# The second MLP's down projection wholly by 7 block products, in parts of 10, 10 and 12 tiles

## The chip, the cores and the metric

One core of one Trainium2 chip. The metric is the device time of one execution in microseconds, as the median of the runs.

## What is computed

Two transformer layers of the older kind (an "even" one with differential and dense attention, an "odd" one with window attention), a final norm, and then one hybrid layer with dilated attention, a state space model and gated units. All data is float32; h has 1024 features and 512 tokens (528 with the meta tokens). The change lies in the odd layer's MLP and at its seam to the hybrid layer:

```python
def _sq_relu_mlp(h, w_up, w_down):
    u = jax.nn.relu(h @ w_up)
    return (u * u) @ w_down

h = h + _sq_relu_mlp(_rmsnorm(h, norm_mlp[i]), w_up[i], w_down[i])    # 1024 -> 4096 -> 1024
h = _rmsnorm(h, norm_final)
return h[:, N_META:]

# the hybrid layer begins with
n = rmsnorm(h, g_mix)
z = n @ w_in
```

## The kernel before

Everything is stored with the features on the 128 partitions and the tokens along a row, so h is 8 tiles of 128x512 (`DT = 8`). A float32 product is made of three matmuls in a rounded type: each operand is split into a rounded half (`_hi`) and the rest (`_lo`), and hi x hi, hi x lo and lo x hi are added in PSUM. A **unit** is one weight tile of 8 x 128x128. SP loads it to `raw` (ring of 4), ScalarE rounds it to `w_hi` (ring of 2, `round_unit`), GpSimd subtracts to get `w_lo` (ring of 2, `low`), TensorE runs 24 matmuls on it. Each engine has its program written out by hand in one function; semaphores with counts tie them together. Nothing reorders the work afterwards.

The second MLP (of the odd layer) has 32 inner tiles of 128. Before, they are treated in two parts of 12 (`up_parts`, `MLP_PARTS = 2`, `PART_SIZES`) and a rest of 8 (`last_up`, `last_down`). For a part:
- *Up.* `project(pj)` makes each inner tile by one unit. VectorE takes it from PSUM with relu and the scale `rstd`, ScalarE squares and rounds it (`round_inner`), VectorE makes four sums of each pair of tiles (`sums_of_pair`), and both split them (`sums_high`, `sums_low`) to `form_hi`, `form_lo`.
- *Down.* `down_by_products` on TensorE, `by_products` on ScalarE and VectorE. The output is treated in four **quads** (`Quad`), each two tiles of h by the two halves of the tokens. A quad is 7 products P1, P2, P5, P6, P3, P4, P7, in this order, in place of the 8 of a 2x2 block product. A product is, for every pair of inner tiles, three matmuls of 128x256: 15 in a part of 10 tiles, 18 in one of 12. Its weights are a block of the matrix or a sum of blocks (VectorE, `weight_sum`), rounded by ScalarE (`product_high`), with the rest by VectorE (`product_low`) or, for P3 and P4, by GpSimd. They lie in a ring of three: `third_hi`/`third_lo` and the two slots of `w_hi`/`w_lo`. VectorE adds each product to h (`keep`).
- In the first quad of a part the last pair of inner tiles is late. So TensorE takes P1, then P2 and P5 with all but the last pair, then the last pair of both.
- `BEHIND[part]` is the unit that follows the part: ScalarE rounds it once the product P3 of the last quad is done (`round_unit`), and the next once P4 is done (`held`).

The rest of 8 tiles is plain. `last_up` makes 8 units into `mr_hi`, `mr_lo`; `last_down` makes the 8 tiles of h with 24 matmuls of 128x512 each. With each finished tile of h, `residual(last_down, 40, True, twice=True)` has ScalarE scale and round it for the hybrid layer (`norm_tile`, L2079) and take two squares of it, with and without the final norm's gain (L2073, L2115). VectorE makes `hr_lo` (L2872) and adds up `sumsq` and `sumsq2` (L2882, L2938). The hybrid layer's projection `middle` starts with `H_LO`, which means that its first unit waits tile by tile for `hr_lo`. Behind this unit `both_stats` adds the squares over the partitions with two matmuls against `ones`; ScalarE's root and VectorE's reciprocal of it scale all that follows. The hybrid layer's gated MLP uses the same block products, in parts of 10 and 12 (`ffn_in`, `ffn_rest`). Its last part already rounds h between its products (`round_residual`, `low_residual`).

## Time and profile before

| | us |
|---|---|
| median of 3 runs | 2095.23 |
| lowest, highest | 2095.11, 2095.38 |
| the profiled execution | 2094.85 |
| its span on the core | 2092.7 |

| engine | busy us | share of the span | instructions |
|---|---|---|---|
| TensorE, matmuls | 2079.1 | 99% | 14278 |
| VectorE | 1355.1 | 65% | 2083 |
| ScalarE | 879.5 | 42% | 1454 |
| GpSimd | 829.0 | 40% | 388 |

The busy time is that of the engine's instructions laid over each other; the span runs from the first instruction to the last. Matmuls are pipelined, so the duration of one in a row is longer than its share of the time: what one costs is the distance between the starts of neighbours. In brackets behind a row stands how long the engine was idle before it, and what it waited for.

### The profile page before, as it was taken

The numbers are of one execution on the slowest core, as the hardware profiler recorded it, in microseconds if no ns is written. First come the engines' busy times: TensorE is split into PE (matmuls) and PEld (weight loads), VectorE is DVE, ScalarE is ACT, GpSimd is POOL, SyncE is SP. The second block draws the span as 40 slices with busy tenths as digits, with TensorE's granted clock in tenths as the row PEclk, the third lists the DMA queues.
The fourth block names the chain that finished last, engine by engine and source line by source line (L and its number), as shares of the span: only waits on it lengthen the run. The fifth ranks groups of instructions, "written<-read, shape, count | busy, mean of one in ns | idle before, by whom it ended". The sixth has DMA issues, their size and how long they took to land.

```text
span 2092.7 us, 35077 instructions
## 1 busy us (share of the span) xinstructions
PE 2079.1 (99%) x14278; PEld 1826.3 (87%) x14278; DVE 1355.1 (65%) x2083; ACT 879.5 (42%) x1454; POOL 829.0 (40%) x388
## 2 busy tenths in 40 slices
PE   9999999999999999999999999999999999999998
PEld 9998899999999777798898788888888788988897
DVE  6678766625723395675855769576774577666865
ACT  5368644223323493443434423344433433433344
POOL 3343434434444453423234443333434443344332
PEclk9999999999999999999999999999999999999999
DMA  6620245233433602323343465233333332433341
GB/s 180 168 59 2 57 136 150 88 117 105 136 91 102 180 2 81 101 87 106 85 117 97 131 136 159 71 84 89 88 91 91 91 94 79 122 91 100 89 122 61
DMA packets 375695, 211.18 MB, mean 101 GB/s; under 512 B 26915, under 2 KB 368132, under 8 KB 374648
## 3 DMA queue, kind: packets, MB, share of 16 engines
q1 hardware_dynamic: 365230, 192.62, 32.6%
q10 hardware_dynamic: 10314, 16.41, 2.8%
q8 instruction: 111, 1.82, 0.4%
q14 instruction: 40, 0.33, 0.1%
HBM read 196.97 MB, written 15.40 MB: 101 GB/s over the span
## 4 chain that ended last, share of the span: by engine, by line
PE 65%; issue 22%; POOL 10%; DVE 2%; ACT 0%; DMA 0%; POOLq 0%; SPq 0%; DVEq 0%; ACTq 0%
PE acc L1268 15%; PE acc L1269 15%; PE acc L1270 14%; POOL w_lo L1038 9%; PE acc L1358 2%; PE ops L1427 2%; PE acc L1679 1%; PE acc L1671 1%; PE acc L1669 1%; PE tps L1367 1%; PE acc L1141 1%; PE ops L1421 1%; PE acc L1142 1%; PE acc L1143 1%; PE tps L1679 1%
## 5 line engine op out<-in xcount | busy, mean ns | idle before, releaser
L1038 POOL TENSOR_TENSOR w_lo<-raw,w_hi 128x1024 fp32r<-128x1024 f32 x278 | 688.2, 2476 | 964.8 <-ACT w_hi L1999 954.3
L1999 ACT ACTIVATE w_hi<-raw 128x1024 fp32r<-128x1024 f32 x277 | 293.4, 1059 | 839.9 <-PE acc L1270 810.5
L1268 PE MATMUL acc<-hr_hi,w_hi 128*128 128x512 f32 x1056 | 421.5, 399 | 0.3 <-POOL w_lo L1038 0.3
L1270 PE MATMUL acc<-hr_hi,w_lo 128*128 128x512 f32 x1056 | 417.7, 396 | 0.0
L1269 PE MATMUL acc<-hr_lo,w_hi 128*128 128x512 f32 x1056 | 417.6, 395 | 0.0
L1268 PE MATMUL acc<-hn_hi,w_hi 128*128 128x264 f32 (+1 forms) x840 | 246.8, 294 | 0.4 <-POOL w_lo L1038 0.4
L1270 PE MATMUL acc<-hn_hi,w_lo 128*128 128x264 f32 (+1 forms) x840 | 244.2, 291 | 0.0
L1269 PE MATMUL acc<-hn_lo,w_hi 128*128 128x264 f32 (+1 forms) x840 | 244.2, 291 | 0.0
L1268 PEld LDWEIGHTS acc<-hr_hi,w_hi 128*128 128x128 f32 x1056 | 198.5, 188 | 48.6 <-issue 1.5
L1270 PEld LDWEIGHTS acc<-hr_hi,w_lo 128*128 128x128 f32 x1056 | 198.4, 188 | 47.9
L1269 PEld LDWEIGHTS acc<-hr_lo,w_hi 128*128 128x128 f32 x1056 | 198.5, 188 | 47.1 <-issue 0.7
L1268 PEld LDWEIGHTS acc<-hn_hi,w_hi 128*128 128x128 f32 x840 | 158.2, 188 | 3.4 <-issue 0.5
L1269 PEld LDWEIGHTS acc<-hn_lo,w_hi 128*128 128x128 f32 x840 | 158.3, 188 | 2.7
L1270 PEld LDWEIGHTS acc<-hn_hi,w_lo 128*128 128x128 f32 x840 | 157.5, 188 | 2.4
L1268 PE MATMUL acc<-mid_hi,w_hi 128*128 128x264 f32 x512 | 145.5, 284 | 0.0
L1269 PE MATMUL acc<-mid_lo,w_hi 128*128 128x264 f32 x512 | 145.0, 283 | 0.0
L1270 PE MATMUL acc<-mid_hi,w_lo 128*128 128x264 f32 x512 | 145.0, 283 | 0.0
L1102 POOL TENSOR_TENSOR w_lo<-blocks,w_hi 128x768 fp32r<-128x768 f32 (+1 forms) x24 | 44.3, 1852 | 138.7 <-ACT w_hi L2404 138.7
L1268 PEld LDWEIGHTS acc<-mid_hi,w_hi 128*128 128x128 f32 x512 | 96.4, 188 | 0.2 <-issue 0.2
L1269 PEld LDWEIGHTS acc<-mid_lo,w_hi 128*128 128x128 f32 x512 | 96.5, 188 | 0.0
L1270 PEld LDWEIGHTS acc<-mid_hi,w_lo 128*128 128x128 f32 x512 | 96.0, 187 | 0.0
L2404 ACT ACTIVATE w_hi<-blocks 128x768 fp32r<-128x768 f32 (+1 forms) x72 | 59.0, 823 | 87.7 <-PE acc L1679 26.9
(551 smaller groups left out, 4389.0 us busy)
## 6 DMA issues: line engine op xcount, KB each, us to landing
raw<-in_w_up SPq DMA_DIRECT2D x64, 512.0 KB, 4.4
raw<-in_w_in SPq DMA_DIRECT2D x56, 512.0 KB, 3.8
raw<-in_w_down SPq DMA_DIRECT2D x40, 512.0 KB, 3.6
blocks<-in_w_down SPq DMA_DIRECT2D x32, 384.0 KB, 3.4
raw<-in_w_ffn_gate SPq DMA_DIRECT2D x22, 512.0 KB, 3.9
raw<-in_w_ffn_up SPq DMA_DIRECT2D x22, 512.0 KB, 3.8
raw<-in_w_in_even SPq DMA_DIRECT2D x18, 512.0 KB, 6.9
blocks<-in_w_ffn_down SPq DMA_DIRECT2D x16, 384.0 KB, 3.5
```

What stands on the lines that cost most here:

```text
L1038: nc.gpsimd.tensor_tensor(w_lo[:, part], raw[:, slot], w_hi[:, part].bitcast(F32), ALU.subtract).then_inc(sems["lo"], T.up("lo"))
L1102: nc.gpsimd.tensor_tensor(lo, block_of(q, PRODUCTS[i][0]), hi.bitcast(F32), ALU.subtract).then_inc(sems["product_lo_pool"], 1)
L1141: mm(out, w_hi[:, part, k, :], x_hi, start=first, stop=False)
L1142: mm(out, w_hi[:, part, k, :], x_lo, start=False, stop=False)
L1268: mm(out, w_hi[:, part, w0 + k, :], xh, start=s0, stop=False)
L1269: mm(out, w_hi[:, part, w0 + k, :], xl, start=False, stop=False)
L1270: ins = mm(out, w_lo[:, part, w0 + k, :], xh, start=False, stop=s1)
L1358: ins = mm(bank[rows, c:c + w], q, keys, start=first, stop=last)
L1427: ins = mm(ops_[b][rows, to], p.v[o][k], weights(o, k)[:, queries], start=k == 0, stop=k == last)
L1679: ins = mm(region(q, i), lo[:, k, :], form_hi[:, form, k, :], start=False, stop=k == pairs - 1, skip_group_check=not opens)
L1999: fn(w_hi[:, n % 2], raw[:, n % 4], ACT.Copy).then_inc(sems["hi"], T.up("hi"))
L2404: fn(weights_of(q, i)[0], block_of(q, role), ACT.Copy).then_inc(sems["product_hi"], 1)
```

## The change

- `PART_SIZES` becomes (10, 10, 12, 10, 12) with `MLP_PARTS = 3`. `last_up` and `last_down` and their buffers are gone: all 32 inner tiles go through block products.
- In the first quad of every part, also of the gated MLP's two, P6's rounded half with all but the last pair comes ahead of the last pairs of P2 and P5; ScalarE rounds P6's weights ahead of the last `sums_high`.
- The third part (`NORM_PART`) does between its products what `last_down` did per tile: scaled rounding of the quad before (`round_gained`, `low_gained`), squares two tiles at a time (`plain_squares`, `gained_squares`) and their sums (`add_plain`, `add_gained`, `fold`). The square tiles lie in `hid_2` and in parts of `form_hi` and `form_lo` that have been read for the last time.
- Behind this part ScalarE rounds two units at once, before the last rounding of h.
- The two matmuls against `ones` move from behind `middle`'s first unit into its second: one ahead of the second k-step, one ahead of the fifth.

```diff
-MLP_PARTS = 2
-PART_SIZES = (PART_TILES, PART_TILES, 10, PART_TILES)
+MLP_PARTS = 3
+PART_SIZES = (10, 10, PART_TILES, 10, PART_TILES)
+NORM_PART, FFN_PART, LAST_PART = MLP_PARTS - 1, MLP_PARTS, MLP_PARTS + 1
...
@@ TensorE
                         for i in (P2, P5):
                             open_product(q, i)
                             high(q, i, most)
                             low(q, i, most)
+                        open_product(q, P6)
+                        high(q, P6, most)
                         for i in (P2, P5):
                             high(q, i, rest)
                             low(q, i, rest)
+                        high(q, P6, rest)
+                        low(q, P6, range(pairs))
...
-            project(last_up)
-            project(last_down, None, ("hidden_lo", LAST_TILES))
...
-            project(middle, None, H_LO, both_stats, after_tile=middle_after)
+            def both_stats(k):
+
+                if k == 1:
+                    pe.wait_ge(sems["gained_sum"], DT // 2)
+                    b = open_("o_")
+                    close(mm(ops_[b][:], ones[:], gained_sums[:, 0], start=True, stop=True), b, "o_")
+                if k == 4:
+                    pe.wait_ge(sems["plain_sum"], DT // 2)
+                    b = open_("o_")
+                    close(mm(ops_[b][:], ones[:], plain_sums[:, 0], start=True, stop=True), b, "o_")
+
+            project(middle, None, H_LO, ahead=[None, both_stats], after_tile=middle_after)
@@ ScalarE
+            def round_gained(q):
+
+                act.wait_ge(sems["product_kept"], q.done(P7))
+                for m in (q.n, q.n + 1):
+                    fn(hr_hi[:, m, :], h[:, m, 0:SEQ], ACT.Copy, scale=gains[:, 40 + m:41 + m]).then_inc(
+                        sems["h_hi"], T.up("h_hi"))
+
+            def plain_squares(n):
+
+                fn(plain[n], h[:, 2 * n:2 * n + 2, 0:SEQ], ACT.Square).then_inc(sems["plain_square"], 1)
...
+            def norm_between(q, i):
+
+                if i == P5 and not q.first:
+                    round_gained(q.before)
+                    if not q.last:
+                        plain_squares(q.n // 2 - 1)
+                if q.last and i == P6:
+                    gained_squares(0)
+                if q.last and i == P3:
+                    gained_squares(1)
+                if q.last and i == P4:
+                    plain_squares(2)
+                if q.last and i == P7:
+                    gained_squares(2)
...
                 act.wait_ge(sems["product"], own[-1].done(P7) - 2)
                 round_unit(BEHIND[part])
-                held[BEHIND[part] + 1] = own[-1].done(P7) - 1
+                if part == NORM_PART:
+                    act.wait_ge(sems["product"], own[-1].done(P7) - 1)
+                    round_unit(BEHIND[part] + 1)
+                    early.append(True)
+                    round_gained(own[-1])
+                    gained_squares(3)
+                    plain_squares(3)
+                else:
+                    held[BEHIND[part] + 1] = own[-1].done(P7) - 1
@@ VectorE
+            def add_gained(n):
+
+                dve.wait_ge(sems["gained_square"], 2 * n + 2)
+                if n > 1:
+                    dve.wait_ge(sems["gained_sum"], n - 1)
+                v.tensor_tensor(gained_sums, gained_sums, gained[n], ALU.add).then_inc(sems["gained_sum"], 1)
...
                     keep(q, P3)
+                    if part == NORM_PART and q.last:
+                        add_plain(1)
...
                     keep(q, P4)
...
+                    if part == NORM_PART and q.last:
+                        add_gained(1)
+                        add_gained(2)
                     keep(q, P7)
+                    if part == NORM_PART and q.last:
+                        add_plain(2)
+                        low_gained(q)
+                        add_gained(3)
+                        fold(gained_sums, "gained_sum")
+                        add_plain(3)
+                        fold(plain_sums, "plain_sum")
```

The order on VectorE at the seam. Before, from the last two tiles of `last_down` to the hybrid layer's first scaling (`acc` is PSUM, `u_t` the first tile of the hybrid layer):

```order
L2929 TENSOR_TENSOR h<-h,acc0 128x512
L2872 SCALAR_TENSOR_TENSOR hr_lo<-h,gains,hr_hi 128x512
L2882 TENSOR_TENSOR sumsq<-sumsq,sq 128x512
L2938 TENSOR_TENSOR sumsq2<-sumsq2,sq2 128x512
L2929 TENSOR_TENSOR h<-h,acc1 128x512
L2872 SCALAR_TENSOR_TENSOR hr_lo<-h,gains,hr_hi 128x512
L2882 TENSOR_TENSOR sumsq<-sumsq,sq 128x512
L2938 TENSOR_TENSOR sumsq2<-sumsq2,sq2 128x512
L3670 RECIPROCAL rstd<-rstd 128x512
L3761 TENSOR_TENSOR u_t<-acc0,rstd 128x64x8
```

In the change, from the keep of P3 in the last quad of the third part (`ops0` is P3's PSUM, `tps` P4's, `acc1` P7's; `hid_2` and `gained0` hold the running sums):

```order
L3541 TENSOR_TENSOR h<-h,ops0 128x256
L3594 TENSOR_TENSOR hid_2<-hid_2 128x1024
L3541 TENSOR_TENSOR h<-h,tps 128x256
L3601 TENSOR_TENSOR gained0<-gained0,gained1 128x1024
L3601 TENSOR_TENSOR gained0<-gained0,gained2 128x1024
L3541 TENSOR_TENSOR h<-h,acc1 128x2x256
L3594 TENSOR_TENSOR hid_2<-hid_2,plain1 128x1024
L3585 SCALAR_TENSOR_TENSOR hr_lo<-h,gains,hr_hi 128x512 x2
L3601 TENSOR_TENSOR gained0<-gained0,gained3 128x1024
L3606 TENSOR_TENSOR gained0<-gained0 128x512
L3594 TENSOR_TENSOR hid_2<-hid_2,plain2 128x1024
L3606 TENSOR_TENSOR hid_2<-hid_2 128x512
```

The two adds of `gained` stand between the keeps of P4 and P7, and one add of `hid_2` between the keep of P7 and the last `hr_lo`.

On ScalarE at the same place, before (each tile: a unit's weights, `hr_hi`, two squares):

```order
L1999 ACTIVATE w_hi<-raw 128x1024
L2079 ACTIVATE hr_hi<-h,gains 128x512
L2073 ACTIVATE sq<-h 128x512
L2115 ACTIVATE sq2<-h,gains 128x512
L2079 ACTIVATE hr_hi<-h,gains 128x512
L2073 ACTIVATE sq<-h 128x512
L2115 ACTIVATE sq2<-h,gains 128x512
L1999 ACTIVATE w_hi<-raw 128x1024
L2676 ACTIVATE rstd<-ops0,small 128x512
L2676 ACTIVATE sq<-ops1,small 128x512
```

and in the change, from the weights of P6 in the last quad on:

```order
L2393 ACTIVATE third_hi<-blocks 128x768
L2428 ACTIVATE gained0<-h,gains 128x512 x2
L2393 ACTIVATE w_hi<-blocks 128x768
L2428 ACTIVATE gained1<-h,gains 128x512 x2
L2393 ACTIVATE w_hi<-blocks 128x768
L2423 ACTIVATE plain1<-h 128x1024
L2393 ACTIVATE third_hi<-blocks 128x768
L2428 ACTIVATE gained2<-h,gains 128x512 x2
L1997 ACTIVATE w_hi<-raw 128x1024 x2
L2418 ACTIVATE hr_hi<-h,gains 128x512 x2
L2428 ACTIVATE gained3<-h,gains 128x512 x2
L2423 ACTIVATE plain2<-h 128x1024
```

The weights of two units now come ahead of the last two `hr_hi`, and squares stand behind each product's weights.

On TensorE in the first quad of a part, from the end of P5's first pairs (`tps` is P2, `ops` P5, `acc` P6), before:

```order
L1679 MATMUL ops<-form_hi,w_lo 128x256 x5
L1669 MATMUL tps<-form_hi,w_hi 128x256
L1671 MATMUL tps<-form_lo,w_hi 128x256
L1679 MATMUL tps<-form_hi,w_lo 128x256
L1669 MATMUL ops<-form_hi,w_hi 128x256
L1671 MATMUL ops<-form_lo,w_hi 128x256
L1679 MATMUL ops<-form_hi,w_lo 128x256
L1669 MATMUL acc<-form_hi,third_hi 128x256
L1671 MATMUL acc<-form_lo,third_hi 128x256
```

and in the change, with the end of P6's first pairs:

```order
L1664 MATMUL acc<-form_hi,third_hi 128x256
L1666 MATMUL acc<-form_lo,third_hi 128x256
L1664 MATMUL acc<-form_hi,third_hi 128x256
L1666 MATMUL acc<-form_lo,third_hi 128x256
L1664 MATMUL tps<-form_hi,w_hi 128x256
L1666 MATMUL tps<-form_lo,w_hi 128x256
L1674 MATMUL tps<-form_hi,w_lo 128x256
L1664 MATMUL ops<-form_hi,w_hi 128x256
L1666 MATMUL ops<-form_lo,w_hi 128x256
L1674 MATMUL ops<-form_hi,w_lo 128x256
L1664 MATMUL acc<-form_hi,third_hi 128x256
L1666 MATMUL acc<-form_lo,third_hi 128x256
```

The last pairs of P2 and P5 now come behind P6's rounded half instead of ahead of it.

## Rows read from the trace of the kernel before

**Rows 1.** The page: its first line, and part 1, busy time by engine

```profile
span 2092.7 us, 35077 instructions
...
PE 2079.1 (99%) x14278; PEld 1826.3 (87%) x14278; DVE 1355.1 (65%) x2083; ACT 879.5 (42%) x1454; POOL 829.0 (40%) x388
```

**Rows 2.** The waits of TensorE, whole span: us in total, times, longest

```profile
PE acc L1268 <- POOL w_lo L1038: 1.1, 3, 0.4
...
PE ops L1669 <- DVE form_lo L3530: 0.8, 1, 0.8
```

**Rows 3.** Busy time by stretch (columns: see the second line)

```profile
core 0: us, PE busy (x) PEld busy (x) DVE busy (x) ACT busy (x) POOL busy (x), PEclk, DMA share, GB/s
902.64:962.16 59.52, 59.52 (x505) 59.52 (x504) 41.38 (x65) 26.21 (x31) 17.71 (x10) 1.00 0.39 109
...
1133.71:1178.49 44.78, 44.78 (x193) 36.06 (x192) 33.43 (x32) 21.87 (x31) 19.26 (x8) 1.00 0.32 93
1776.49:1827.36 50.87, 49.77 (x421) 49.36 (x420) 38.01 (x66) 22.93 (x30) 15.63 (x10) 1.00 0.41 113
```

**Rows 4.** Timeline, TensorE, first quad of the gated part (start, us, engine, line, ...)

```profile
1781.43 0.28 PE L1679 MATMUL tps<-form_hi,w_lo 128*128 128x256 f32 x1
1782.55 0.39 PE L1669 MATMUL ops<-form_hi,w_hi 128*128 128x256 f32 x1 [0.85 <-DVE form_lo L3530]
```

**Rows 5.** Timeline, VectorE, same quad

```profile
1781.28 1.22 DVE L3530 TENSOR_TENSOR form_lo<-pair_sums,form_hi 128x1024 fp32r<-128x1024 f32 x1
1782.42 0.82 DVE L3506 TENSOR_TENSOR third_lo<-blocks,third_hi 128x640 fp32r<-128x640 f32 x1
```

**Rows 6.** Timeline, TensorE: first matmul behind the second part, and behind the gated part

```profile
1088.91 0.39 PE L1268 MATMUL acc<-hr_hi,w_hi 128*128 128x512 f32 x1
...
1827.37 0.47 PE L1268 MATMUL acc<-hr_hi,w_hi 128*128 128x512 f32 x1 [0.26 <-POOL w_lo L1038]
```

**Rows 7.** Timeline, ScalarE, end of the second part

```profile
1084.87 1.06 ACT L1999 ACTIVATE w_hi<-raw 128x1024 fp32r<-128x1024 f32 x1 [1.23 <-PE ops L1679]
1086.99 1.06 ACT L1999 ACTIVATE w_hi<-raw 128x1024 fp32r<-128x1024 f32 x1 [1.06 <-PE tps L1679]
```

**Rows 8.** Timeline, GpSimd, end of the second part

```profile
1086.01 4.78 POOL L1038 TENSOR_TENSOR w_lo<-raw,w_hi 128x1024 fp32r<-128x1024 f32 x2 [2.54 <-ACT w_hi L1999]
```

**Rows 9.** Timeline, VectorE, end of the second part

```profile
1084.87 0.42 DVE L3525 TENSOR_TENSOR h<-h,ops 128x256 f32<-128x256 f32 x1 [0.24 <-PE ops L1679]
1086.99 0.42 DVE L3525 TENSOR_TENSOR h<-h,tps 128x256 f32<-128x256 f32 x1 [1.70 <-PE tps L1679]
1089.11 0.69 DVE L3525 TENSOR_TENSOR h<-h,acc 128x512 f32<-128x512 f32 x1 [1.70 <-PE acc L1679]
```

**Rows 10.** Timeline, VectorE, then GpSimd, one up projection

```profile
1014.81 2.58 DVE L3530 TENSOR_TENSOR form_lo<-pair_sums,form_hi 128x1024 fp32r<-128x1024 f32 x1 [1.35 <-ACT form_hi L2409]
...
1026.19 1.21 DVE L3530 TENSOR_TENSOR form_lo<-pair_sums,form_hi 128x1024 fp32r<-128x1024 f32 x1
...
1013.90 2.41 POOL L1038 TENSOR_TENSOR w_lo<-raw,w_hi 128x1024 fp32r<-128x1024 f32 x1 [3.20 <-ACT w_hi L1999]
```

**Rows 11.** Timeline, VectorE, then GpSimd, end of the gated up projections

```profile
1945.84 4.03 DVE L3499 TENSOR_TENSOR blocks<-blocks 128x768 f32<-128x768 f32 x2
...
1946.37 2.68 POOL L1038 TENSOR_TENSOR w_lo<-raw,w_hi 128x1024 fp32r<-128x1024 f32 x1 [3.07 <-ACT w_hi L1999]
```

**Rows 12.** Timeline, VectorE, then GpSimd, second quad of the second gated part

```profile
1981.39 1.22 DVE L3560 TENSOR_TENSOR hr_lo<-h,hr_hi 128x1024 fp32r<-128x1024 f32 x1
1982.53 0.95 DVE L3506 TENSOR_TENSOR w_lo<-blocks,w_hi 128x768 fp32r<-128x768 f32 x1
...
1982.42 2.76 POOL L1102 TENSOR_TENSOR w_lo<-blocks,w_hi 128x768 fp32r<-128x768 f32 x1 [9.71 <-ACT w_hi L2404]
```

**Rows 13.** Timeline, ScalarE, then VectorE, last tile of last_down

```profile
1179.43 0.72 ACT L2079 ACTIVATE hr_hi<-h,gains 128x512 fp32r<-128x512 f32 x1 [3.52 <-DVE h L2929]
...
1180.18 0.75 DVE L2872 SCALAR_TENSOR_TENSOR hr_lo<-h,gains,hr_hi 128x512 fp32r<-128x512 f32 x1 [0.79 <-ACT hr_hi L2079]
```

More of the change, by code:

```diff
@@ L495, in transposed_blocks_program @@
             att_lo = sb(s, "att_lo", [P, 4, SEQ], F32R)
+        FORM, FORMS_LO = PART_PAIRS * SEQ // 2, 7 * PART_PAIRS * SEQ // 2
+        gained = [over(at, (f"gained{n}", [P, 2, SEQ]))[0] for n, at in enumerate((SEQ, FORMS_LO, FORM, 2 * FORM))]
+        plain = [plain_sums, hid_2[:, 0]] + [over(FORMS_LO + n * FORM, (f"plain{n}", [P, 2, SEQ]))[0] for n in (1, 2)]
+        gained_sums = gained[0]
         bb, = over(34 * LEN, ("bb", [P, 2, 16, 16]))
@@ L2757, in middle_tile @@
                     fn(mixed_hi[:, n, :], G[:, 0, :], ACT.Copy).then_inc(sems["mixed_hi"], T.up("mixed_hi"))
-            project(middle, middle_tile, own=[t for t, x in enumerate(MID) if x[0] == "glu_b"], first=both_stats)
+            project(middle, middle_tile, own=[t for t, x in enumerate(MID) if x[0] == "glu_b"], second=both_stats)
             residual(out_2, 48, True)
@@ L3587, in by_products @@
                             low_residual(q.before)
+                        if part == NORM_PART:
+                            low_gained(q.before)
                     product_low(q, P6)
```

113 lines of the change are left out of this document (41 added, 72 removed).

## Prediction

> **What bounds the kernel now.** I read the page's totals first: TensorE is busy 99% of a 2092.7 us span [rows 1]. The list of waits on that engine then says how much of the span it stands still at all. In the whole kernel it has one wait of 0.8 us for a `form_lo` tile and three of 1.1 us together for a `w_lo` tile [rows 2]; the rest is as small. So time comes off this kernel only where TensorE gets fewer or shorter instructions, and anything on VectorE, ScalarE or GpSimd costs nothing until a matmul waits for it. The table of stretches prices the two kinds of matmul. The granted clock is 1.00 (2.4 GHz) in all of them. 504 block matmuls of 256 columns took 59.52 us, 0.1181 us each, and the 192 plain matmuls of `last_down` took 44.78 us, 0.2333 us each [rows 3]. The ten-tile part of the gated MLP is the one place where the block form already shows stalls: 50.87 us for 420 matmuls, where 420 x 0.1181 is 49.60, so 1.3 us are waits [rows 3].
>
> **The change, part by part.** In what follows M is the moment at which the layer behind a part starts on TensorE (1088.91 behind the second part of before [rows 6]).
>
> *Matmuls.* The up projections keep 32 tiles. The down product had 2 x 504 block matmuls and 192 plain ones. Now it has 420 + 420 + 504 = 1344 block matmuls. Added: 336 x 0.1181 = 39.7 us. Removed: 44.8 us. Net -5.1 us, all on the path. The two sums with `ones` stay, two products of two passes each, only later in the program: 0.
>
> The Trainium skill speaks against this trade: TensorE: Matmul & The Clock Gate, section Back-to-back issue gap, gives about 81 ns for a sustained matmul of 128 columns with its weight load and 131 ns for one of 512, so that halving the columns saves far less than half. An estimate between its two figures, 98 ns at 256 columns, would make this part 336 x 0.098 - 192 x 0.131 = +7.8 us. The trace disagrees with it at both widths [rows 3], and the measurement decides.
>
> *Ends of the ten-tile parts.* ScalarE rounds the next unit's weights once the product P3 is done and GpSimd subtracts behind it. In a twelve-tile part this starts 4.04 us before M [rows 7, 6] and the first GpSimd subtraction, half of 4.78 us from M - 2.90, ends 0.5 us before it is needed [rows 8]. With ten tiles the two products behind P3 last 0.7 us less (2 x 3 matmuls), and the first matmul behind the gated part did wait 0.26 us for that subtraction [rows 6]. I take 0.35 us for each of parts one and two (0.26 to 0.5): +0.7 us.
>
> *First quads.* P6's rounded half with all but the last pair now runs ahead of the last pairs of P2 and P5. That covers 8 matmuls, 0.9 us, in a ten-tile part. The gated part waited 0.85 us for `form_lo` (with the slower matmuls about it, 1.0) [rows 4, 5]. With the cover, the low part of P6 is next: VectorE's subtraction for it runs 0.82 us from 1782.42 [rows 5], to 6.8 us behind the start, and TensorE wants it at 6.5. So that part gets back about 0.6 of its 1.0 us. What is pushed back is the end of P2, and with it ScalarE's rounding and GpSimd's 1.6 to 1.85 us subtraction for P3. In a ten-tile MLP part I work this out as 0.25 us of wait. In a twelve-tile one P2 now ends 1.2 us later and P3's low part is some 0.4 us late where nothing was late before. Parts: +0.25 +0.25 +0.35 (the third), -0.6 (first gated), +0.1 (second gated): +0.3 us, between -0.6 and +1.5.
>
> *Inside the third part's quads.* For each quad ScalarE gets two scaled roundings (0.72 us each by the row of `hr_hi` [rows 13]) and about 1.06 us of squares behind P5's weights. It has 2.1 us for each product and needs 0.85 for its weights, so P6's weights start at most 0.8 us late with more than 2 us in hand: 0. VectorE gets two `hr_lo` of 0.75 us where the second gated part has one of 1.22 us [rows 12, 13], 0.3 us more. P6's subtraction then stands near the moment at which GpSimd asks for its own [rows 12]. I take +0.2 us for all quads (0 to 1.8).
>
> *From the last quad into the next layer.* Here is the largest unknown. VectorE and GpSimd do not overlap when both read two SBUF operands. A 128x1024 subtraction takes 1.21 us alone and 2.58 us when it begins 0.9 us into GpSimd's 2.41 us: it ended 1.1 us behind GpSimd's end [rows 10]. Additions into PSUM-fed `h` are untouched beside GpSimd, at 0.42 us [rows 9, 8]. The order in VectorE's program is now: keep P3, add squares (1024 wide), keep P4, two more such adds, keep P7, one more add, then the two `hr_lo`. Placed on the rows of before:
> - keep P3 is at M - 4.0, so the first add runs from M - 3.7 to M - 2.5. GpSimd asks at M - 2.9 and holds the port from M - 2.5 to M - 0.1: just in time for TensorE.
> - keep P4 is at M - 1.9 [rows 9]. The second add comes at M - 1.6, finds the port taken and ends at M + 1.0.
> - GpSimd's next subtraction has been ready since M - 0.1. Where VectorE issued a second two-operand instruction while GpSimd already asked, GpSimd went in between (two 0.95 us instructions took 4.03 us [rows 11]). So: GpSimd to M + 3.4, the third add to M + 4.5, and keep P7 to M + 5.1 where it was done at M + 0.9 [rows 9].
> - ScalarE's `hr_hi` of the last two tiles follow at M + 5.8 and M + 6.4; VectorE's add and `hr_lo` end at M + 6.9 and M + 7.6.
> - TensorE wants the seventh tile after 18 matmuls, at M + 4.2. It waits 2.8 us. The sum of squares (two roundings, two squares, an add, a fold) is ready at M + 9.5 and wanted at M + 9.1: 0.4 us more.
>
> If VectorE holds the port for both adds instead, keep P7 ends at M + 2.7, but then the add before `hr_lo` runs into GpSimd, and the same chain gives 2.1 + 0.4 us. I take +3.0 us (0 if nothing meets on the port, 3.4 at most).
>
> The Trainium skill, SBUF — State Buffer, section Who interferes with whom, says that whichever of the two issues first gets the shared port pair for its whole instruction. By that rule the waiting second add goes ahead of GpSimd's next subtraction and the third behind it, which is the first of my two orders; no row of before shows GpSimd with two in a row and VectorE waiting. The sum by the rule would be 0.2 us above mine.
>
> **Sum:** -5.1 + 0.7 + 0.3 + 0.2 + 3.0 = -0.9 us. The profiled execution took 2094.85 us, its span 2092.7; so 2093.95. The median of the runs is 2095.23, 0.38 above it: I forecast 2094.3.
>
> **Rivals.**
> - *No meeting on the port (chance 0.25).* For it: every add is only 1.2 us and stands in a gap of 1.7 us between two keeps. Against: GpSimd's 2.4 us fills that gap. Without it keep P7 ends at M + 0.9, the add at M + 2.0 and the `hr_lo` at M + 2.7 and M + 3.4, ahead of the 4.2 and 4.9 at which they are wanted, and the squares' sum at M + 5.2 ahead of 6.3. -5.1 + 0.7 + 0.3 + 0.1 = -4.0: 2091.2.
> - *The full arithmetic (0.05).* Early P6 also clears the new first-quad waits and the part ends cost little: -5.1, 2090.1.
> - *Slower: VectorE loses the port in the quads too (0.12).* If its subtraction for P6 is asked for more than about 0.2 us behind GpSimd's for P3, it waits for 1.85 us. In the second gated part the two lie 0.11 us apart [rows 12], and the new quads bring 0.3 us more work ahead of it. P6's low half would be 0.6 us late in each of three quads (+1.8 for +0.2), the first quads 0.8 us worse, the end 0.4 us worse. It makes -0.9 + 1.6 + 0.8 + 0.4 = +1.9: 2097.1. It decides from the point where these waits together pass 5.1 us.
> - *It does not do what it says:* the built order shows the plain matmuls gone and the squares in the quads, so no chance.
>
> **How the numbers follow.** The forecast with its own spread (2093.3 to 2095.3) has 0.58. The range reaches over the no-meeting case and half of the slower one: 2090.9 to 2096.2. A measurement of this kernel can tell about 0.2%, 4.2 us, from no change. The no-meeting case at -4.0 is on that line: two fifths of it and the full arithmetic, with a little for errors of mine, make 0.17 for faster. Slower by 4.2 us needs the slower case and more: 0.03. The rest, 0.80, is within.
>
> **What would show it.** Right: TensorE's wait list gains one of 2 to 3 us for `hr_lo` in the layer's first unit and a shorter one for the squares' sum; VectorE's two adds of `gained` take 2 us and more each; keep P7 starts 2 to 4 us late; the 420-matmul stretches last 50.2 us. Wrong: if `hr_lo` is never waited for, the port chain was wrong and the time is near 2091; if the quads of the third part last over 60.5 us, the slower rival holds; if block matmuls are not at 0.118 us, the first term is wrong.

## The result, and the profile of the changed kernel

| | before | changed |
|---|---|---|
| median of 20 runs each, same chip | 2095.17 us | 2097.59 us |
| ratio, 95% interval | | 1.0014 [1.0008, 1.0021] |
| profiled execution, span | 2094.85, 2092.7 us | 2097.81, 2096.0 us |

The change made the kernel 2.4 us slower. By the 0.2% that I called the smallest difference to be told it is no change; the interval is narrower than that and lies wholly above 1. The forecast was 2094.3, the range ended at 2096.2, so the time is outside it. The profile shows one execution of each kernel, so its spans differ by 3.3 us where the medians differ by 2.4.

The first rows of the page, against [rows 1]: TensorE is busy 0.4 us longer, though its matmuls should last 5.1 us less, and the span is 3.3 us longer. So most of the loss lies in what counts as busy.

```profile
span 2096.0 us, 35502 instructions
...
PE 2079.5 (99%) x14422; PEld 1831.6 (87%) x14422; DVE 1383.7 (66%) x2149; ACT 891.2 (43%) x1474; POOL 829.2 (40%) x388
```

The waits of TensorE, whole span (us in total, times, longest). The `form_lo` wait of [rows 2] is gone. A wait of 2.3 us for `hr_lo` is new. So are short ones for weights (`w_lo` at L1033 and L1097) and for `h`.

```profile
PE acc L1263 <- DVE hr_lo L3585: 2.3, 1, 2.3
...
PE acc L1263 <- POOL w_lo L1033: 1.0, 5, 0.2
...
PE ops L1674 <- POOL w_lo L1097: 0.4, 2, 0.2
...
PE acc L1664 <- DVE h L3541: 0.3, 1, 0.3
```

The table of stretches: the three parts of the second MLP (compare [rows 3]), then four stretches at the start of the layer behind them (its first matmul is at 1176.54, the M of the forecast).

```profile
core 0: us, PE busy (x) PEld busy (x) DVE busy (x) ACT busy (x) POOL busy (x), PEclk, DMA share, GB/s
891.49:942.26 50.77, 50.46 (x421) 49.80 (x420) 37.16 (x65) 23.35 (x31) 15.64 (x10) 1.00 0.42 114
998.34:1049.09 50.75, 50.44 (x421) 49.78 (x420) 37.16 (x65) 23.35 (x31) 15.65 (x10) 1.00 0.43 114
1116.36:1176.54 60.18, 59.90 (x505) 59.51 (x504) 48.47 (x73) 35.97 (x46) 20.91 (x10) 1.00 0.39 108
...
1180.60:1183.30 2.70, 0.38 (x2) 0.00 (x0) 2.70 (x5) 1.80 (x3) 0.00 (x0) 1.00 0.68 194
1183.30:1184.60 1.30, 1.28 (x5) 1.02 (x6) 1.13 (x2) 1.30 (x3) 0.00 (x0) 0.97 0.00 0
1184.60:1187.30 2.70, 2.70 (x8) 1.69 (x6) 2.63 (x4) 1.47 (x2) 0.85 (x1) 0.50 0.03 6
1187.30:1190.00 2.70, 2.70 (x11) 1.75 (x9) 2.70 (x2) 0.69 (x1) 2.12 (x1) 0.88 0.00 0
```

What to see: the down product took 50.77 + 50.75 + 60.18 = 161.7 us. Before it was 59.54 + 59.55 + 44.80 = 163.9 (the first two are 504 matmuls each, as in [rows 3]). That is 2.2 us less, where 5.1 us less of matmul time was forecast. 1344 x 0.118 is 158.6, so 3.1 us are waits. Then one matmul starts at 1180.58 and the next at 1183.32: TensorE is idle for 2.34 us. It starts again at full clock, and 1.3 us later the granted clock falls to 0.50 (1.2 GHz) for 2.7 us. Below I call this stop the gap; the recorded texts count it as 2.7 us, from start to start.

From M to the first transposes of the new layer there are 192 matmuls of eight units. They lasted from 1178.50 to 1225.01 before, 46.51 us, and from 1176.54 to 1228.08 now, 51.54 us: 5.03 us more. The first transposes, before and now:

```profile
1225.01 0.60 PE L1328 MATMUL tps<-ident,qkv 128*128 128x128 f32 x4
...
1228.08 0.60 PE L1323 MATMUL tps<-ident,qkv 128*128 128x128 f32 x4
```

The two parts of the gated MLP took 0.15 and 0.22 us more. Together -2.2 + 5.0 + 0.4 = +3.2 of the span's 3.3 us.

TensorE at that place (start, us, engine, line, ...):

```profile
1183.32 0.50 PE L1263 MATMUL acc<-hr_hi,w_hi 128*128 128x512 f32 x1 [2.34 <-DVE hr_lo L3585]
...
1185.08 0.63 PE L1263 MATMUL acc<-hr_hi,w_hi 128*128 128x512 f32 x1
...
1186.36 1.80 PE L1884 MATMUL ops<-gained,ones 128*128 128x512 f32 x2
1187.28 1.11 PE L1263 MATMUL acc<-hr_hi,w_hi 128*128 128x512 f32 x1
...
1190.09 1.06 PE L1888 MATMUL ops<-hid,ones 128*128 128x512 f32 x2
...
1194.37 0.50 PE L1263 MATMUL acc<-hr_hi,w_hi 128*128 128x512 f32 x1 [0.43 <-DVE u_t L3806]
```

VectorE, then GpSimd, in the same stretch:

```profile
1174.73 6.13 DVE L3601 TENSOR_TENSOR gained<-gained 128x1024 f32<-128x1024 f32 x2
1180.79 0.68 DVE L3541 TENSOR_TENSOR h<-h,acc 128x512 f32<-128x512 f32 x1
...
1182.52 1.40 DVE L3585 SCALAR_TENSOR_TENSOR hr_lo<-h,gains,hr_hi 128x512 fp32r<-128x512 f32 x2
...
1185.36 0.69 DVE L3606 TENSOR_TENSOR gained<-gained 128x512 f32<-128x512 f32 x1
1185.97 1.22 DVE L3594 TENSOR_TENSOR hid<-hid,plain 128x1024 f32<-128x1024 f32 x1
1187.22 2.75 DVE L3606 TENSOR_TENSOR hid<-hid 128x512 f32<-128x512 f32 x1
1189.89 3.34 DVE L3715 RECIPROCAL rstd<-rstd 128x512 f32<-128x512 f32 x1
1193.27 1.05 DVE L3806 TENSOR_TENSOR u_t<-acc,rstd 128x512 f32<-128x512 f32 x1
...
1173.41 6.37 POOL L1033 TENSOR_TENSOR w_lo<-raw,w_hi 128x1024 fp32r<-128x1024 f32 x2 [1.53 <-ACT w_hi L1997]
...
1186.45 2.97 POOL L1033 TENSOR_TENSOR w_lo<-raw,w_hi 128x1024 fp32r<-128x1024 f32 x1 [6.67 <-ACT w_hi L1997]
```

The first row is the forecast meeting: two adds of 1.2 us took 6.13 us beside two subtractions of GpSimd that took 6.37 instead of 4.78 [rows 8]. The rest of the list is what I did not follow to its end: behind the gained fold come a plain add and the plain fold, the fold 2.75 us for its 0.69 beside GpSimd's next subtraction, and only then the reciprocal that every `u_t` needs. The third unit of the layer waits for the first `u_t`, since it takes over that tile's accumulator. The same two steps in the kernel before, and the start of its third unit on TensorE:

```profile
1185.88 3.35 DVE L3670 RECIPROCAL rstd<-rstd 128x512 f32<-128x512 f32 x1 [3.74 <-ACT rstd L2676]
1189.27 1.09 DVE L3761 TENSOR_TENSOR u_t<-acc,rstd 128x512 f32<-128x512 f32 x1
...
1191.41 0.40 PE L1268 MATMUL acc<-hr_hi,w_hi 128*128 128x512 f32 x1
```

There the first `u_t` was done at 1190.36 and the third unit began at 1191.41: 1.05 us in hand. Behind M the reciprocal ended at +10.73 (1185.88 + 3.35 - 1178.50) before and at +16.69 now, 5.96 us later. Less the 1.05 in hand that is 4.9 us, the seam's loss to 0.1 us. That the third unit starts behind the first `u_t` is in the row; the experiments had to show whether the time follows from it, or from the gap and the clock.

### The profile page after: what moved, and what is told of

Read it like the earlier page. It is cut to its first block, busy times and chain, and to the rows that moved or that the text cites. A ratio compares the mean times of both kernels' runs of the same rounds, so it can differ in the third digit from the quotient of the medians.

```text
span 2096.0 us, 35502 instructions
## 1 busy us (share of the span) xinstructions
PE 2079.5 (99%) x14422; PEld 1831.6 (87%) x14422; DVE 1383.7 (66%) x2149; ACT 891.2 (43%) x1474; POOL 829.2 (40%) x388
## 4 chain that ended last, share of the span: by engine, by line
PE 66%; issue 20%; POOL 10%; DVE 3%; ACT 1%; POOLq 0%; DMA 0%; DVEq 0%; ACTq 0%
PE acc L1263 15%; PE acc L1264 15%; PE acc L1265 15%; POOL w_lo L1033 8%; PE acc L1353 2%; PE ops L1422 2%; POOL w_lo L1097 1%; PE acc L1664 1%; PE acc L1666 1%; PE tps L1362 1%; PE ops L1416 1%; PE acc L1136 1%; PE acc L1674 1%; PE acc L1138 1%; PE acc L1137 1%
## 5 line engine op out<-in xcount | busy, mean ns | idle before, releaser
L1033 POOL TENSOR_TENSOR w_lo<-raw,w_hi 128x1024 fp32r<-128x1024 f32 x270 | 671.6, 2488 | 937.6 <-ACT w_hi L1997 926.8
L1997 ACT ACTIVATE w_hi<-raw 128x1024 fp32r<-128x1024 f32 x269 | 285.2, 1060 | 810.5 <-PE acc L1265 778.5
L1097 POOL TENSOR_TENSOR w_lo<-blocks,w_hi 128x640 fp32r<-128x640 f32 (+1 forms) x30 | 56.5, 1893 | 165.6 <-ACT w_hi L2393 165.6
L2393 ACT ACTIVATE w_hi<-blocks 128x640 fp32r<-128x640 f32 (+1 forms) x90 | 70.0, 784 | 108.3 <-PE acc L1674 24.0
```

The costliest lines, as they stand in the source:

```text
L1033: nc.gpsimd.tensor_tensor(w_lo[:, part], raw[:, slot], w_hi[:, part].bitcast(F32), ALU.subtract).then_inc(sems["lo"], T.up("lo"))
L1097: nc.gpsimd.tensor_tensor(lo, block_of(q, PRODUCTS[i][0]), hi.bitcast(F32), ALU.subtract).then_inc(sems["product_lo_pool"], 1)
L1997: fn(w_hi[:, n % 2], raw[:, n % 4], ACT.Copy).then_inc(sems["hi"], T.up("hi"))
L2393: fn(weights_of(q, i)[0], block_of(q, role), ACT.Copy).then_inc(sems["product_hi"], 1)
```

## The experiments

Each was timed in 11 runs, the kernel before 21 or 33 times on the same chip, with medians of 2094.85 to 2095.09. The ratios are to that kernel. Experiments 1 to 4, 5 to 8, 9 and 10, and 11 and 12 were made on four different chips, and the changed kernel was not timed again beside them: a difference to its 2097.59 goes across chips. All intervals are some 0.09% (1.9 us) to either side, so smaller differences of the medians rest on the traces.

**1. The two adds ahead of P7's keep left out** (the gained sum is then without the squares of four tiles; the counts that wait for these adds are lowered to fit).

```diff
-                    if part == NORM_PART and q.last:
-                        add_gained(1)
-                        add_gained(2)
```

> The change without VectorE's two adds of gained squares between the keeps of P4 and P7 in the third part's last quad; their terms are missing from one sum of squares. Port theory (these two adds wait behind GpSimd and so hold back the keep of P7 and the last hr_lo): the 2.7 us gap in the hybrid layer's first unit goes, and with it the matmuls at 0.43 us and the late start of the third unit, some 4.5 to 5 us in all: about 2093. Rival (the chain from the last product over ScalarE's rounding to hr_lo is itself too long to be covered by six tiles of matmuls): a gap of 1.5 us or more stays, 2096 or more.

Measured: 2094.97 us, ratio 0.9999 [0.9990, 1.0008]. The gap before the seventh tile and the slow matmuls are gone. So the two adds, with all that their meeting with GpSimd brings, cost 2.6 us by the medians and 3.0 us at the seam (first transposes at M + 48.57 for 51.54). The run takes out the adds and the meeting together and does not price them apart. The time stayed 2 us above the 2093 expected: the third unit still waited, because the reciprocal still came late, behind the plain sums:

```profile
1184.18 2.77 DVE L3604 TENSOR_TENSOR hid<-hid 128x512 f32<-128x512 f32 x1
1186.88 3.34 DVE L3710 RECIPROCAL rstd<-rstd 128x512 f32<-128x512 f32 x1
```

**2. P6 of the first quads in its place of before.**

```diff
-                        open_product(q, P6)
-                        high(q, P6, most)
                         for i in (P2, P5):
                             high(q, i, rest)
                             low(q, i, rest)
-                        high(q, P6, rest)
-                        low(q, P6, range(pairs))
...
-                        whole(q, P6)
-                    for i in (P3, P4, P7):
+                    for i in (P6, P3, P4, P7):
```

ScalarE's rounding of P6's weights goes back behind the last `sums_high` with it.

> The change with the order of the first quads of before: P6 behind the last pairs of P2 and P5. Theory of the forecast (early P6 covers the wait for form_lo in ten-tile parts): without it each ten-tile part loses about 0.6 us, the twelve-tile parts win 0.3 to 0.4 each: +1.1 us net, 2098.7. Rival, from the trace of the change (what it covers comes back as a wait for P3's low half and for the second quad's P2): ten-tile parts within 0.2 us of the change, twelve-tile parts 0.4 us less each, 2096.8.

Measured: 2096.86 us, ratio 1.0008 [0.9999, 1.0017]. The quads took 50.85, 50.55 and 59.54 us, against 50.77, 50.75 and 60.18. So with ten tiles the early P6 takes away one wait for `form_lo` (0.60 us idle, 0.86 with the slower matmuls about it) and gives the same back: 0.24 us at P3's low weights, 0.40 at P2's in the second quad, 0.21 at P5's last pair. With twelve tiles there was nothing to take away, and it costs 0.6 us. That is the rival of the expectation, not the forecast's theory. The ten-tile gated part took 51.19 us here, 51.04 in the changed kernel.

**3. The gap filled with 10 spare matmuls on `ones`.**

```diff
+            def fill(k):
+                if k == 6:
+                    for _ in range(10):
+                        mm(ops_[1][:, 0:P], ones[:], ones[:], start=True, stop=True)
...
-            project(middle, None, H_LO, ahead=[None, both_stats], after_tile=middle_after)
+            project(middle, None, H_LO, ahead=[fill, both_stats], after_tile=middle_after)
```

> The change with 10 spare matmuls of 128 columns against ones (float32, two passes each, into an unused bank) at the place where TensorE waits for the seventh tile's hr_lo. The wait stays as long. Clock theory (the granted clock falls to 1.2 GHz because TensorE stood still): the matmuls behind stay at 0.23 us and the sums against ones at 0.43 us a pass, 1.7 to 2 us less: about 2095.8. Rival (the slow matmuls are no matter of standing still): as slow as in the change, 2097.6, or more by what the spare matmuls outlast the wait.

Measured: 2097.67 us, ratio 1.0015 [1.0006, 1.0024], no gain at all. The table of stretches of this kernel, for the same four stretches:

```profile
1180.60:1183.30 2.70, 2.59 (x22) 2.40 (x21) 2.70 (x5) 2.02 (x4) 0.00 (x0) 1.00 0.67 194
1183.30:1184.60 1.30, 1.30 (x6) 0.99 (x6) 1.12 (x2) 1.30 (x2) 0.00 (x0) 1.00 0.00 0
1184.60:1187.30 2.70, 2.28 (x8) 1.24 (x7) 2.63 (x4) 1.51 (x3) 1.36 (x1) 1.00 0.00 0
```

The clock stays at 1.00, so it was the standing still that had let it fall. The expected 1.7 to 2 us did not come: the matmuls, now faster, came to VectorE's results too early. TensorE in this kernel:

```profile
1185.89 1.12 PE L1884 MATMUL ops<-gained,ones 128*128 128x512 f32 x2 [0.42 <-DVE gained L3612]
...
1189.82 1.12 PE L1888 MATMUL ops<-hid,ones 128*128 128x512 f32 x2 [0.72 <-DVE hid L3612]
...
1194.16 0.50 PE L1263 MATMUL acc<-hr_hi,w_hi 128*128 128x512 f32 x1 [0.43 <-DVE u_t L3812]
```

M is 1176.33 here, so the third unit starts at M + 17.83, to 0.01 us where it started in the changed kernel. The slow clock had cost nothing here: it lay in the shadow of VectorE's chain.

**4. The kernel before, with the early P6 alone.**

> The kernel before with P6 early in the first quads, alone (parts of 12, 12, 10, 12). By the trace of the change: the ten-tile part no better (0.0 to +0.2 us), the three twelve-tile parts 0.3 to 0.45 us longer each: +1.1 us, 2096.3. By the forecast: -0.6 for the ten-tile part and +0.1 to +0.4 for the others: 2095.2 to 2095.6.

Measured: 2096.31 us, ratio 1.0007 [0.9998, 1.0016]; the first two twelve-tile parts took 59.93 us each instead of 59.54, the ten-tile gated part 51.24 instead of 50.89, the last part 49.32 instead of 49.15. In the twelve-tile parts it agrees in sign with the second experiment (0.4 us here; there 0.6, of which 0.2 is a wait at the part's end that these two do not have). In the ten-tile gated part it does not: 0.35 us lost here, 0.15 won there. The early P6 gained nothing in either.

**5. VectorE's order changed, all sums kept.**

```diff
                     keep(q, P3)
-                        add_plain(1)
+                        add_gained(1)
...
                     keep(q, P4)
-                        add_gained(1)
-                        add_gained(2)
                     keep(q, P7)
-                        add_plain(2)
                         low_gained(q)
+                        add_gained(2)
                         add_gained(3)
                         fold(gained_sums, "gained_sum")
+                        add_plain(1)
+                        add_plain(2)
                         add_plain(3)
                         fold(plain_sums, "plain_sum")
```

> All sums are kept; in the last quad of the third part VectorE's order is changed: the first gained add in the place of the first plain one (before GpSimd's two subtractions begin), no add in front of P7's keep, the other two gained adds, the fold, and then all three plain adds and their fold behind the low parts of the residual, ahead of the reciprocal. Port theory (the two adds in front of P7's keep took 6.13 us beside GpSimd and made the 2.7 us gap at k = 6 of the first unit): the gap shrinks to under 0.5 us and no matmul runs at 427 ns. Chain theory (VectorE's whole list of sums, the plain ones with it, stands in front of the reciprocal that u_t needs): the third unit of the middle projection then waits over 2 us for u_t, since four plain additions of some 4.5 us now stand ahead of the reciprocal, and the time is 2096.5 to 2098, no better than the changed kernel. If only the gap counted, it would be 2094.5.

Measured: 2098.19 us, ratio 1.0015 [1.0006, 1.0024]: no better, as the chain theory said, but not where it said. The gap is gone, and the wait stands at the plain ones product (3.3 us), not at the third unit. The reciprocal ends at M + 16.46, 0.2 us earlier than in the changed kernel. Behind the wait the granted clock fell to 0.50 for 2.8 us, against the expectation, and the second unit ended so late that the first `u_t` was done 1.0 us before the third unit began.

**6. The last plain add, the plain fold and the plain ones product behind the first `u_t`.**

```diff
                         fold(gained_sums, "gained_sum")
-                        add_plain(3)
-                        fold(plain_sums, "plain_sum")
...
+                if m == 0:
+                    add_plain(3)
+                    fold(plain_sums, "plain_sum")
```

> The changed kernel with the last plain add and the plain fold behind the reciprocal and the first u_t, and the plain ones product (with its square root) one unit later. Chain theory: the reciprocal starts about 2 to 3 us earlier (the fold of 2.75 us beside GpSimd no longer stands ahead of it), u_t is there in time, the third unit's wait of 0.43 and 0.1 us goes, and the time falls by 0.5 us against the changed kernel; the gap of 2.7 us and the matmuls at 427 ns stay, since the gained adds stand where they stood. Rival (only the gap counts): no difference, within 0.2 us.

The new lines stand in `chunked`, behind the store of `u_t`; the plain ones product moves from the second unit to the third. Measured: 2097.22 us, ratio 1.0010 [1.0001, 1.0019], 0.4 us under the changed kernel; the two intervals overlap, so this alone tells little. The reciprocal starts 1.0 us earlier behind M, not 2 to 3. It now waited for its square root, since the gained ones product ran at the halved clock. By the timeline the clock cost something here; no run tests it. The third unit starts at M + 16.88, 0.95 us earlier, and the first transposes at M + 51.44, only 0.10 earlier: the plain ones product now stands behind the third unit's start and costs its 0.86 us there.

**7. Both edits (5 and 6).**

> Both edits together, all sums kept. Chain theory: neither the gap, nor slow matmuls, nor the wait of the third unit; what is left of the seam are the two interruptions by the ones products (about 0.7 us each): 2097.6 less 2.7 for the gap less about 1 for the slow matmuls and the wait, 2093.5 to 2094.5. Rival (the loss at the seam is the ones products and the waits of the low parts themselves, whatever the order): over 2095.5.

Measured: 2097.31 us, ratio 1.0011 [1.0002, 1.0020]. Expected were 2093.5 to 2094.5, so I had not understood it yet. VectorE of this kernel, then TensorE:

```profile
1184.08 3.23 DVE L3603 TENSOR_TENSOR hid<-hid,plain 128x1024 f32<-128x1024 f32 x1
1187.23 3.34 DVE L3721 RECIPROCAL rstd<-rstd 128x512 f32<-128x512 f32 x1
...
1191.69 0.80 PE L1263 MATMUL acc<-hr_hi,w_hi 128*128 128x512 f32 x1 [2.78 <-DVE u_t L3816]
1192.28 0.63 PE L1264 MATMUL acc<-hr_lo,w_hi 128*128 128x512 f32 x1
```

The gap at the seventh tile is gone, and a stop of the same size stands at the third unit. A plain add met GpSimd's next subtraction and took 3.23 us ahead of the reciprocal, and the slow matmuls came back with the stop (granted clock 0.50 from 1191.7 to 1194.4, seven matmuls, some 1.4 us).

**8. The same with the late P6.**

> The same with P6 of the first quads back in its place of before (the version meant to be the best of both). Since the earlier P6 cost about 0.6 us in the twelve-tile part and something like 0.2 in the others, 0.7 us less than the kernel with both edits: 2092.8 to 2094. That is 1 to 2 us under the kernel before. If the two effects do not add, the same time as with both edits.

Measured: 2096.69 us, ratio 1.0008 [0.9999, 1.0018]. Against its sister 0.6 us less, inside the intervals of both but of the size of experiment 2, and not the level expected (2092.8 to 2094). The same wait of 2.8 us stands at its third unit.

**9. Experiment 8 with only one plain add ahead of the reciprocal, the other two behind the first `u_t`.** The plain ones product stands at the end of the third unit.

> The kernel with both edits and the late P6, but with only the first plain add ahead of the reciprocal; the second, which took 3.23 us beside GpSimd's subtraction in that kernel, goes behind the first u_t with the third and the fold, and the plain ones product to the last k of the third unit. Chain theory: the square root is ready 1.2 us after the gained ones product, so the reciprocal starts 2.4 us earlier, u_t lands within 0.5 us of the end of the second unit, the third unit's wait falls from 2.8 to about 0.4 us, and the matmuls at 427 ns behind it (1.2 us in all) go: about 3.4 us off the profiled span of 2093.8, so 2090 to 2091, and a median of 2092.5 to 2094. Rival (the third unit waits for something else, a bank or its weights): the wait stays over 2 us, and the time does.

Measured: 2098.25 us, ratio 1.0016 [1.0007, 1.0025]. The reciprocal came 2.4 us earlier and the third unit waited 0.37 us, both as expected, but the expected 2092.5 to 2094 was missed by 4 us. The wait had moved once more. VectorE, then TensorE:

```profile
1191.41 2.78 DVE L3609 TENSOR_TENSOR hid<-hid 128x512 f32<-128x512 f32 x1
...
1195.03 1.01 DVE L3809 TENSOR_TENSOR u_t<-acc,rstd 128x512 f32<-128x512 f32 x1
...
1216.73 0.50 PE L1263 MATMUL acc<-hr_hi,w_hi 128*128 128x512 f32 x1 [2.27 <-DVE qkv L3835]
```

The adds now stand ahead of the second `u_t`, which is done 7.1 us behind the first (in the kernel before 2.4), and all that VectorE has to do from there, the angle tables above all, is late with it, up to a wait of 2.27 us for the first `qkv` tile. Behind that wait the granted clock fell to 0.50 for 2.7 us, which cost some 1.6 us more in the profiled execution; at 2099.84 us that one is 1.6 above the median.

**10. The same with one gained add ahead of P7's keep.**

> The same, with the second gained add in front of P7's keep, where VectorE stands idle for 1.7 us. Beside GpSimd one add takes about 3 us, so P7's keep is late by 0.6 to 1.3 us and the low parts with it; they are due at k = 6 of the first unit, 4.2 us behind its start, and were done 0.7 us before that. Chain theory: the gained fold is 0.6 us earlier or the same, and the unit's k = 6 waits 0 to 0.6 us: within 0.5 us of the kernel without this step, either way. If it waits over 1 us, one add there is already too much.

Measured: 2097.73 us, ratio 1.0014 [1.0005, 1.0023], 0.5 us below its sister. The add took 2.45 us, P7's keep was 0.6 us late, and no matmul waited for it. One add there is harmless, two are not. The wait for `qkv` is as long as in experiment 9, but here the granted clock stayed at 1.00 behind it:

```profile
1216.45 0.50 PE L1263 MATMUL acc<-hr_hi,w_hi 128*128 128x512 f32 x1 [2.26 <-DVE qkv L3836]
```

**What they had in common.** Read off the timelines of VectorE and TensorE, behind each kernel's own M:

| kernel | reciprocal ends | third unit starts | 4th `u_t` done | first transposes |
|---|---|---|---|---|
| before | 10.73 | 12.91 | 26.39 | 46.51 |
| changed | 16.69 | 17.83 | 31.43 | 51.54 |
| 1, adds left out | 13.74 | 14.87 | 28.45 | 48.57 |
| 3, filled | 16.70 | 17.83 | 31.40 | 51.53 |
| 5, gained order | 16.46 | 18.58 | 32.06 | 52.18 |
| 7, both | 14.40 | 15.52 | 31.02 | 51.46 |
| 9, reciprocal first | 11.85 | 13.00 | 32.49 | 53.53 |
| 10, one add ahead | 11.50 | 12.64 | 32.09 | 51.57 |
| 11, below | 11.52 | 12.66 | 26.25 | 47.50 |

Where no add stands between the reciprocal and the fourth `u_t` (before, changed, 1, 3), that `u_t` is done 14.7 to 15.7 us behind the reciprocal's end, and the transposes follow 20.1 us behind it. My reading at this point was that VectorE's own list sets the pace up to the fourth `u_t`, and that a sum anywhere on it ahead of that point moves the wait and not the end. That made the test of experiment 11.

The table says it more exactly. From the third unit to the transposes lie six units, 144 matmuls or 33.6 us. In the kernel before, the changed one, 1, 3 and 5 the last column is 33.6 to 33.7 us above the second: TensorE waited for nothing there, and all they lose or win lies in the start of the third unit. In 7 it is 35.9, but no matmul waits for VectorE there either: the 2.3 us are the halved clock (1.4) and the plain ones product (0.9), which now lies in this stretch. Only in 9 and 10 do the adds behind the first `u_t` hold TensorE up behind the third unit's start, at the third and fourth `u_t` and at `qkv` (0.5 + 0.3 + 2.3 us idle in both). So a sum ahead of the reciprocal is paid at the third unit, and one between the first `u_t` and the fourth at the units behind.

**11. No plain add but the first ahead of the fourth `u_t`.** The plain sum lies in other memory, the third squares are taken behind the last rounding of weights, and the last two adds and the fold run behind the fourth `u_t`, where VectorE had stood idle; the plain ones product goes into the sixth unit. The rest is experiment 10, and the cut of the diff is against it.

```diff
-                if m == 0:
+                if m == 3:
                     add_plain(2)
                     add_plain(3)
                     fold(plain_sums, "plain_sum")
...
-            project(middle, None, H_LO, ahead=[None, both_stats, plain_stats], after_tile=middle_after)
+            project(middle, None, H_LO, ahead=[None, both_stats, None, None, None, plain_stats], after_tile=middle_after)
```

> The two kernels before this one moved the wait and not the end: in every kernel with the block products up to the last tile, the fourth u_t ends 14.7 us behind the end of the reciprocal plus what VectorE adds in between, and the first transposes of the new layer begin 20.1 us behind the fourth u_t. So the theory is now: VectorE, not TensorE, sets the first 27 to 32 us of the new layer, and every sum that stands on VectorE ahead of the fourth u_t lengthens it. Here none but the first plain add is left there: the plain sum lies in other memory, its last two adds and its fold run behind the fourth u_t, where VectorE stands idle 2.9 us for the sines, and the plain ones product in the sixth unit. P6 is late, one gained add stands ahead of P7's keep. Theory: reciprocal ends 11.5 us behind the layer's start, fourth u_t at 26.3 to 27, first transposes at 46.4 to 47.2 us (51.5 in the changed kernel, 46.5 in the kernel before); median 2091.8 to 2093. Rival (the loss belongs to the ones products and the clock, wherever VectorE's adds stand): over 49 us and over 2095.

Measured: **2092.86 us, ratio 0.9989 [0.9980, 0.9998]**, profiled span 2091.2. It is 4.7 us under the changed kernel and 2.2 under the kernel before, with all the arithmetic of the change. The interval lies wholly below 1, though the difference to the kernel before is also within the 0.2%. Against experiment 10 the reciprocal and the third unit come at the same time (11.5 and 12.7 us behind M), and the first transposes 4.1 us earlier: that much the adds behind the first `u_t` had cost. VectorE in it:

```profile
1184.13 3.35 DVE L3715 RECIPROCAL rstd<-rstd 128x512 f32<-128x512 f32 x1 [0.80 <-ACT rstd L2699]
1187.52 1.05 DVE L3808 TENSOR_TENSOR u_t<-acc,rstd 128x512 f32<-128x512 f32 x1
...
1201.12 1.09 DVE L3808 TENSOR_TENSOR u_t<-acc,rstd 128x512 f32<-128x512 f32 x1
1202.05 4.03 DVE L3597 TENSOR_TENSOR plain_sums<-plain_sums,plain 128x1024 f32<-128x1024 f32 x2
...
1207.50 2.59 DVE L3802 COPY rope_c<-rstd 128x512 f32<-128x512 f32 x1
```

M is 1175.96. The reciprocal's end (+11.52) and the fourth `u_t` (+26.25) came where the expectation put them; the transposes came at +47.50, 0.3 us behind the expected 47.2. The moved adds take 4.03 us for 2.4 beside GpSimd, and the copy behind them is held up as well.

**12. The same with the early P6.**

> The same with P6 of the first quads where the change has it, so that against the changed kernel only the seam differs. If the two effects add, 0.3 to 0.8 us above its sister kernel with the late P6: 2092.3 to 2093.6, and 4 to 5 us under the changed kernel. If the time is that of the sister, the early P6 costs nothing once the seam is mended.

Measured: 2093.24 us, ratio 0.9992 [0.9983, 1.0001]; quads 50.53, 50.75 and 60.11 us, first transposes at M + 47.62. Against the changed kernel only the seam differs: 4.4 us by the medians, 3.9 us from M to the transposes. That is what VectorE's order there was worth. The early P6 costs 0.4 us by the medians, less than their intervals can tell; the 0.6 us of the third part (60.11 for 59.55) is in the traces.

## Why the prediction was wrong, step by step

- **Matmuls, -5.1: held.** Block matmuls ran at 0.118 us wherever nothing was waited for (59.54 and 59.55 us for 504 in experiments 2 and 11). The 98 ns that I had estimated from the Trainium skill, TensorE: Matmul & The Clock Gate, section Back-to-back issue gap, do not show in any run.
- **Ends of the ten-tile parts, 0.35 each: held**, 0.34 to 0.36 us. The end of the twelve-tile part cost 0.22 us where I had 0; the kernel with the late P6 has no such wait there.
- **First quads, +0.3: wrong, by 2 us.** The gated part was to get 0.6 us back and lost 0.15: the `form_lo` wait went, and P6, opened earlier, waited 0.3 us for P1's keep, whose accumulator it takes, and P3's low weights and the second quad's took the rest. The two ten-tile MLP parts were to lose 0.25 us each and lost 0.8 each (50.77 less 49.60 and less the 0.35 of the end); I had written down 50.2 us for them. The third lost 0.4, the last 0.2. I had costed the cover and not what the cover itself waits for.
- **Inside the third part's quads, +0.2: nothing there.** Without the early P6 the part takes 59.54 us, as in the kernel before with no residual work in it, so the slower rival (VectorE loses the port in the quads) did not happen. Its 2097.1 lies near the measured 2097.6 by chance.
- **The last quad and the next layer, +3.0: this step failed; it was +5.0.** Its first half held nearly to the digit: keep P7 to end at M + 5.1 (it ended at M + 4.9), `hr_lo` at M + 7.6 (M + 7.4), a wait of 2.8 us (2.5 more than the usual distance of two starts), the gained sum at M + 9.5 (M + 9.5). The order on the port was the one I took: VectorE's waiting add, GpSimd's second subtraction, then the third add. The keep's time decides it, since with both adds ahead of the second subtraction it would have ended at M + 2.7. By the Trainium skill, SBUF — State Buffer, section Who interferes with whom, the order comes out so too, and the keep at M + 4.9 agrees. What failed is where I stopped, at "ready at M + 9.5 and wanted at M + 9.1: 0.4 us more". The sum is wanted for the ones product, but behind it stand the square root, 3.3 us of reciprocal and the first `u_t`, and the third unit waits for that. It had 1.05 us in hand, which rows of the kernel before would have shown, and I did not price what the change puts ahead of the reciprocal: 1.22 and 2.75 us of plain sum. The gap is not paid on top of that: experiments 5 and 7 removed it, kept the list ahead of the fourth `u_t`, and had their transposes at M + 52.18 and M + 51.46, against 51.54. Experiments 11 and 12 took the sums off that list and had them at 47.50 and 47.62. The signs that I had named for being right nearly all came (a wait of 2.3 us for `hr_lo`, the two adds at 3 us each, the keep 4 us late) while the time was outside the range: none of them looked past the first wait.
- **The granted clock** was in no term. It fell to 0.50 behind the gap, and by experiment 3 this cost nothing there. In 5, 6, 7 and 9 the timelines show a cost of about 1 to 1.6 us; there it is read off and not tested.
- **The list of waits ahead of the sum** was read too shortly: besides `form_lo` and `w_lo` the kernel before has waits of 1.9 us for `sq` and 1.1 us for `sq_tok` on TensorE. They are the same in the changed kernel, so no term hangs on it.

In sum: -2.2 us for the quads (forecast -3.3 with the ends), +0.4 for the gated MLP (-0.5), +5.0 for the seam (+3.0). The seam is half of the miss. With it as forecast the time would have been about 2095.6, inside the range; what it would still be above the forecast is the first quads.

## What to carry to other kernels

When work moves from one stage's shadow into the next stage's start, follow each engine there until the first result that TensorE takes over a buffer for, not only to the first wait, and write down how much each such result has in hand. If an order change removes a wait and the time stays, look for the engine whose list is as long as before; here only taking work off that list ahead of its last deadline helped. Check, too, from which point on the waiting engine itself never waits: behind it nothing is lost any more. An add of 1.2 us that met GpSimd's weight subtraction took 2.5 to 3.2 us in these runs.

## What the runs showed of the hardware that was new to me

- Two adds of VectorE (1.21 us each alone) against two GpSimd subtractions (2.4 us each alone) took 6.13 and 6.37 us: both queues were held up. An instruction with one operand is held as well: the copy to `rope_c` took 2.59 us beside GpSimd in experiment 11 and 0.41 in the kernel before. P7's keep, fed from PSUM (0.67 us), and the reciprocal (3.35 us) ran beside GpSimd there at their usual length.
- After 2.34 us of idling TensorE went on at a granted clock of 1.00 (2.4 GHz), and only 1.3 us later was it 0.50 (1.2 GHz) for 2.7 us: matmuls of 0.427 instead of 0.233 us. With 20 small passes in the gap the clock stayed at 1.00. The delay differs from stop to stop: behind the waits of 2.8 us in experiments 7 and 8 matmuls ran at 0.427 us at once, behind 3.3 us in experiment 5 0.6 us later, behind 2.27 us in experiment 9 0.4 us later, and behind 2.26 us in experiment 10 the clock did not fall.
- At full clock a ones product of two passes takes 0.45 to 0.56 us of TensorE, and from the start of the matmul behind it to the next are 0.63 us instead of 0.23: each interruption costs some 0.9 to 1.0 us, and two side by side, as before the change, 1.7. Moved elsewhere, it costs the same there (experiments 6 and 7).
